# Latent and differential heads of a hybrid trunk on Trainium2: mask rows, packed values, rotation on GpSimd, and moved splits, evictions and fills

## The reference, cut to what matters

```python
# latent heads (B): keys of 64 + 32 dimensions, values of 64
s = (einsum(q_nope, k_nope) + einsum(q_rope, k_rope)) * scale
p = softmax(where(k_chunk <= q_chunk, s, -inf))      # chunks of 64 frames
out_b = einsum(p, v)
# differential heads (A): two score maps, values of 128
q, k = rope(rms_norm(q), pos), rope(rms_norm(k), pos)
p = softmax(s1) - lam * softmax(s2)                  # both masked by chunk
out_a = rms_norm(einsum(p, v)) * (1 - lam0)
x = x + concat(out_a, out_b) @ w_out
```

## Time and profile before

| | us |
|---|---|
| median of three executions | 1278.57 |
| lowest and highest | 1277.1, 1279.0 |
| profiled execution | 1279.58 |
| its span, first to last instruction | 1277.8 |
| TensorE busy | 1253.7 |
| ScalarE busy | 583.9 |
| VectorE busy | 569.3 |
| GpSimd busy | 528.7 |

### The profile page before, as it was taken

How to read it: one execution, slowest core, us unless ns; L and a number is a source line. 1 busy time by engine, 2 the same in 40 slices (tenths; PEclk the granted TensorE clock), 3 DMA queues, 4 the chain that set the end, 5 groups by cost and what they waited for, 6 DMA issues and landing times.

```text
span 1277.8 us, 16943 instructions
## 1 busy us (share of the span) xinstructions
PE 1253.7 (98%) x6308; PEld 1064.7 (83%) x6308; DVE 569.3 (45%) x995; ACT 583.9 (46%) x959; POOL 528.7 (41%) x267
## 2 busy tenths in 40 slices
PE   8999989999999999999999999999999999999999
PEld 8899968888888888888878888887888888888887
DVE  7856568553221022222288887887232210122210
ACT  5767756454322122223377878885443221222320
POOL 4656411175445344445432222222744444344442
PEclk9999989999999999999999999999999999999999
DMA  5221100033333222232221111110332332222331
GB/s 204 88 66 51 51 34 19 15 128 101 97 117 114 71 95 97 90 123 94 74 66 50 49 49 66 61 55 17 115 99 99 106 119 75 96 92 92 118 118 42
DMA packets 29143, 105.84 MB, mean 83 GB/s; under 512 B 3360, under 2 KB 3616, under 8 KB 29088
## 3 DMA queue, kind: packets, MB, share of 16 engines
q1 hardware_dynamic: 28944, 105.07, 24.8%
q10 hardware_dynamic: 144, 0.02, 0.0%
HBM read 102.98 MB, written 2.10 MB: 82 GB/s over the span
## 4 chain that ended last, share of the span: by engine, by line
PE 88%; DVE 8%; ACT 1%; issue 1%; POOL 1%; DMA 0%; POOLq 0%
PE bank L346 23%; PE bank L347 22%; PE bank L350 22%; PE bank L1512 3%; PE bank L1543 2%; PE bank L1459 1%; PE bank L1125 1%; PE bank L966 1%; PE bank L970 1%; PE bank L968 1%; PE bank L1074 1%; PE bank L1364 1%; PE bank L1365 1%; PE bank L1054 1%; PE bank L372 1%
## 5 line engine op out<-in xcount | busy, mean ns | idle before, releaser
L335 POOL TENSOR_TENSOR w_lo<-wraw,w_hi 128x1024 fp32r<-128x1024 f32 (+4 forms) x180 | 456.8, 2539 | 687.1 <-ACT w_hi L323 687.1
L346 PE MATMUL bank<-h_hi,w_hi 128*128 128x512 f32 x896 | 350.9, 392 | 0.1
L347 PE MATMUL bank<-h_lo,w_hi 128*128 128x512 f32 x896 | 349.0, 389 | 0.0
L323 ACT ACTIVATE w_hi<-wraw 128x1024 fp32r<-128x1024 f32 (+4 forms) x180 | 198.2, 1102 | 243.6 <-DVE x L671 125.6
L350 PE MATMUL bank<-h_hi,w_lo 128*128 128x512 f32 x896 | 221.8, 389 | 0.0
L346 PEld LDWEIGHTS bank<-h_hi,w_hi 128*128 128x128 f32 x896 | 168.2, 188 | 36.2 <-issue 1.1
L350 PEld LDWEIGHTS bank<-h_hi,w_lo 128*128 128x128 f32 x896 | 168.2, 188 | 34.9
L347 PEld LDWEIGHTS bank<-h_lo,w_hi 128*128 128x128 f32 x896 | 168.3, 188 | 34.3
L346 PE MATMUL bank<-f_hi,w_hi 128*128 128x512 f32 x352 | 136.9, 389 | 0.0
L347 PE MATMUL bank<-f_lo,w_hi 128*128 128x512 f32 x352 | 136.9, 389 | 0.0
L634 ACT ACTIVATE f_hi<-fa 128x512 f32 (+1 forms) x44 | 27.8, 633 | 217.2 <-DVE fa L660 217.2
(11 more groups left out here) (281 smaller groups left out, 1995.6 us busy)
## 6 DMA issues: line engine op xcount, KB each, us to landing
wraw<-in_w_in SPq DMA_DIRECT2D x120, 512.0 KB, 3.2
wraw<-in_w_down SPq DMA_DIRECT2D x32, 704.0 KB, 4.1
wraw<-in_w_ab SPq DMA_DIRECT2D x20, 512.0 KB, 3.3
x<-in_xt SPq DMA_DIRECT2D x8, 256.0 KB, 6.0
out<-x SPq DMA_DIRECT2D x8, 256.0 KB, 2.0
wraw<-in_w_ab SPq DMA_DIRECT2D x4, 416.0 KB, 6.0
wraw<-in_w_ab SPq DMA_DIRECT2D x2, 384.0 KB, 3.1
wraw<-in_w_ab SPq DMA_DIRECT2D x2, 256.0 KB, 2.8
```

Of the source, the lines that this page charges most:

```text
L323: nc.scalar.activation(whi[:, s, at:at + width], wraw[:, s, at:at + width], ACT.Copy).then_inc(S("w_hi"), 1)
L335: nc.gpsimd.tensor_tensor(wlo[:, s, at:at + width], wraw[:, s, at:at + width], whi[:, s, at:at + width], ALU.subtract).then_inc(S("w_lo"), 1)
L346: nc.tensor.matmul(out_bank, w, src_hi[kt], start=(kt == 0), stop=False)
L347: nc.tensor.matmul(out_bank, w, src_lo[kt], start=False, stop=False)
```

## The change

Masks: `masks_a` gets a second part of 512 columns in partitions 96 to 127. Of the 32, eight rows hold, on the query side, 1 where the frame is in chunk c and, on the key side, -1e30 where the key's chunk is later than c. They are written once into the spare partitions of `bqhi` and `bkhi` (zeros into those of `bqlo` and `bklo`), the latent scores contract over 128 rows instead of 96, and the four mask matmuls of a head are gone. The differential heads keep theirs.

Packed values: `vb` holds for each head 64 high columns beside 64 low ones. The first matmul gives high x high in output rows 0 to 63 and low x high in 64 to 127, the second adds high x low to rows 0 to 63. ScalarE copies the lower half to `bo`, VectorE adds the upper, and the sum is split from `bo` one head later.

Rotation: ScalarE squares and copies a projected half from the accumulator; VectorE only sums the squares; GpSimd makes all three products and the add (`qk_rope_pool`), in heads 1, 3, 5, 6. Both halves of a group are now evicted in the same head, for the value groups too. The differential transposes wait for all four rotations. `k_scale_pool` runs in heads 5 and 7.

Differential heads: zero fills on GpSimd in head 7, `T_L0` on ScalarE (`a_l0_act`), the split of chunk 22 + u after the transposed probabilities.

```diff
-    (vbhi, vblo), _ = pair("vb", [P, NB, B_HEADS * B_V])
+    vb, _ = place("vb", [P, NB, B_HEADS, 2 * B_V], F32R)
...
+    bo, end = place("bo", [P, SEQ], F32, at=r0)
...
-            act.wait_ge(S("cmask"), 1)
+            act.wait_ge(S("cmask"), 5)
...
-        c = slice(256 * hf, 256 * hf + 256)
-        nc.scalar.activation(vbhi[:, i, c], bank[KV_BANK[n % 3]][:, 256:512], ACT.Copy)
+        nc.scalar.activation(vb[:, i, 4 * hf:4 * hf + 4, 0:B_V],
+                             bank[KV_BANK[n % 3]][:, 256:512].rearrange("p (h n) -> p h n", h=4), ACT.Copy)
...
-        nc.vector.tensor_tensor(vblo[:, i, c], b[:, 256:512], vbhi[:, i, c], ALU.subtract).then_inc(S("bv_lo"), 1)
+        heads = slice(4 * hf, 4 * hf + 4)
+        nc.vector.tensor_tensor(vb[:, i, heads, B_V:2 * B_V], b[:, 256:512].rearrange("p (h n) -> p h n", h=4),
+                                vb[:, i, heads, 0:B_V], ALU.subtract).then_inc(S("bv_lo"), 1)
...
+        nc.scalar.activation(qk_of(p)[0][:, p % 2, 2 * t:2 * t + 2, :],
+                             bank[PJ[t]][:].rearrange("p (i n) -> p i n", i=2), ACT.Copy).then_inc(S("pj_c"), 1)
...
-    def qk_dve(dve, p, t):
-
+    def qk_sum_dve(dve, p, t):
+
+        dve.wait_ge(S("pj_sq"), 2 * p + t + 1)
+        nc.vector.reduce_sum(col(t_as(p) + 8 * t, 8), pj_sq[:, t, :].rearrange("p (j n) -> p j n", n=A_DIM),
+                             AX).then_inc(S("pj_sum"), 1)
...
+    ROPE_AT = (1, 3, 5, 6)
+
+    def qk_rope_pool(pool, p):
         dst, tab = qk_of(p)
...
+        o = dst[:, p % 2, :, :].rearrange("p i (j n) -> p i j n", n=A_DIM)
+        u = t2[:].rearrange("p (i j n) -> p i j n", i=NB, n=A_DIM)
...
-        nc.vector.tensor_tensor(u[:, :, :, 0:s], y[:, :, :, s:2 * s], of(A_DIM, s), ALU.mult)
-        nc.vector.tensor_tensor(u[:, :, :, s:2 * s], y[:, :, :, 0:s], of(A_DIM + s, s), ALU.mult)
-        nc.vector.tensor_tensor(o, y, of(0, A_DIM), ALU.mult).then_inc(S("pj_c"), 1)
-        nc.vector.reduce_sum(col(t_as(p) + 8 * t, 8), pj_sq[:, t, :].rearrange("p (j n) -> p j n", n=A_DIM),
-                             AX).then_inc(S("pj_sum"), 1)
...
-    def qk_add_pool(pool, p):
+            return spread(tab[:, :, a:a + w].rearrange("p i (j n) -> p i j n", j=1), [P, NB, 4, w])
         pool.wait_ge(S("pj_c"), 2 * p + 2)
-        dst, _ = qk_of(p)
-        o = dst[:, p % 2, :, :].rearrange("p i n -> p (i n)")
-        nc.gpsimd.tensor_tensor(o, o, t2[:], ALU.add).then_inc(S("pj_add"), 1)
+        wait(pool, "pj_add", p)
+        nc.gpsimd.tensor_tensor(u[:, :, :, 0:s], o[:, :, :, s:2 * s], of(A_DIM, s), ALU.mult).then_inc(S("pj_t"), 1)
+        nc.gpsimd.tensor_tensor(u[:, :, :, s:2 * s], o[:, :, :, 0:s], of(A_DIM + s, s), ALU.mult).then_inc(S("pj_t"), 1)
+        pool.wait_ge(S("pj_t"), 3 * p + 2)
+        nc.gpsimd.tensor_tensor(o, o, of(0, A_DIM), ALU.mult).then_inc(S("pj_t"), 1)
+        pool.wait_ge(S("pj_t"), 3 * p + 3)
+        nc.gpsimd.tensor_tensor(o, o, u, ALU.add).then_inc(S("pj_add"), 1)
...
+            pe.wait_ge(S("cmask"), 5)
...
             for n, (a, c) in enumerate(((bqhi, bkhi), (bqhi, bklo), (bqlo, bkhi))):
-                nc.tensor.matmul(o, a[0:B_QK, b * P:(b + 1) * P], c[0:B_QK, 0:w], start=(n == 0), stop=False,
-                                 skip_group_check=True)
-            last = nc.tensor.matmul(o[:, w - 256:w], ident_r[:], cmask[:, 0 if b == 0 else 1, :], start=False,
-                                    stop=True, skip_group_check=True)
+                last = nc.tensor.matmul(o, a[:, b * P:(b + 1) * P], c[:, 0:w], start=(n == 0), stop=(n == 2),
+                                        skip_group_check=True)
...
     def b_values_pe(pe, u, kb):
         pe.wait_ge(S("h_plo"), 3 * u + min(kb + 1, 3))
         if kb == 0:
-            wait(pe, "h_mlo", u)
-        c = slice(P * (u // 2), P * (u // 2) + P)
-        for n, (a, t) in enumerate(((vbhi, pthi), (vbhi, ptlo), (vblo, pthi))):
-            last = nc.tensor.matmul(bank[OUT][:, TQ[kb]:SEQ], a[:, kb, c], t[:, V_AT[kb]:V_AT[kb] + TW[kb]],
-                                    start=(kb == 0 and n == 0), stop=(kb == NB - 1 and n == 2))
+            wait(pe, "b_add", u)
+        for n, (rows, t) in enumerate(((P, pthi), (B_V, ptlo))):
+            last = nc.tensor.matmul(bank[OUT][0:rows, TQ[kb]:SEQ], vb[:, kb, u, 0:rows],
+                                    t[:, V_AT[kb]:V_AT[kb] + TW[kb]], start=(kb == 0 and n == 0),
+                                    stop=(kb == NB - 1), skip_group_check=True)
         if kb == NB - 1:
             last.then_inc(S("h_o"), 1)
 
-    def b_out_act(act, u):
+    def b_rows(u):
+        return slice(64 * (u % 2), 64 * (u % 2) + 64)
+
+    def b_lower_act(act, u):
         act.wait_ge(S("h_o"), u + 1)
-        r = slice(64 * (u % 2), 64 * (u % 2) + 64)
-        nc.scalar.activation(mhi[r, A_HEADS + u // 2, :], bank[OUT][r, :], ACT.Copy).then_inc(S("h_mhi"), 1)
-
-    def b_out_dve(dve, u):
+        wait(act, "h_mlo", u - 1)
+        nc.scalar.activation(bo[b_rows(u), :], bank[OUT][B_V:P, :], ACT.Copy).then_inc(S("b_lower"), 1)
+
+    def b_add_dve(dve, u):
+        dve.wait_ge(S("b_lower"), u + 1)
+        r = b_rows(u)
+        nc.vector.tensor_tensor(bo[r, :], bank[OUT][0:B_V, :], bo[r, :], ALU.add).then_inc(S("b_add"), 1)
+
+    def b_mhi_act(act, u):
+        act.wait_ge(S("b_add"), u + 1)
+        r = b_rows(u)
+        nc.scalar.activation(mhi[r, A_HEADS + u // 2, :], bo[r, :], ACT.Copy).then_inc(S("h_mhi"), 1)
+
+    def b_mlo_dve(dve, u):
         dve.wait_ge(S("h_mhi"), u + 1)
-        r = slice(64 * (u % 2), 64 * (u % 2) + 64)
-        nc.vector.tensor_tensor(mlo[r, A_HEADS + u // 2, :], bank[OUT][r, :], mhi[r, A_HEADS + u // 2, :],
+        r = b_rows(u)
+        nc.vector.tensor_tensor(mlo[r, A_HEADS + u // 2, :], bo[r, :], mhi[r, A_HEADS + u // 2, :],
                                 ALU.subtract).then_inc(S("h_mlo"), 1)
...
+                pe.wait_ge(S("a_zero"), 4)
...
-        if c == 2:
-            l0 = tiny[:, T_L:T_L + 8:2]
-            nc.vector.scalar_tensor_tensor(col(T_L0, NB), l0, EPS, l0, ALU.mult, ALU.mult).then_inc(S("a_l0"), 1)
+
+    def a_l0_act(act, u):
+        act.wait_ge(*at_a("e", 8 * u + 8))
+        nc.scalar.activation(col(T_L0, NB), tiny[:, T_L:T_L + 8:2], ACT.Square, scale=EPS ** 0.5).then_inc(S("a_l0"), 1)
...
-                pe.wait_ge(S("h_mlo"), B_HEADS)
+                pe.wait_ge(S("b_add"), B_HEADS)
...
-        pe.wait_ge(S("pj_add"), u // 2 + 1)
+        pe.wait_ge(S("pj_add"), 4)
...
-    def a_zero_dve(dve):
-
-        dve.wait_ge(S("h_s"), 3 * B_HEADS)
-        for t in (aqhi, aqlo):
-            nc.vector.memset(t[64:128, 0, :].bitcast(F32), 0.0)
-            nc.vector.memset(t[0:64, 1, :].bitcast(F32), 0.0)
+    def a_zero_pool(pool):
+
+        pool.wait_ge(S("h_s"), 3 * B_HEADS)
+        pool.wait_ge(S("pj_add"), 4)
+        pool.wait_ge(S("w_lo"), 14 + B_HEADS - 1)
+        for n, t in enumerate((aqhi, aqlo)):
+            nc.gpsimd.memset(t[64:128, 0, :].bitcast(F32), 0.0).then_inc(S("a_zero"), 1)
+            pool.wait_ge(S("a_zero"), 2 * n + 1)
+            nc.gpsimd.memset(t[0:64, 1, :].bitcast(F32), 0.0).then_inc(S("a_zero"), 1)
+            pool.wait_ge(S("a_zero"), 2 * n + 2)
...
+            sp.dma_start(rawm[:, :, 0:256], masks_a[:, :, 0:256]).then_inc(S("masks_in"), 16)
+            sp.dma_start(rawm[B_QK:P, :, 256:], masks_a[B_QK:P, :, 256:]).then_inc(S("masks_in"), 16)
...
-            qk_add_pool(pool, 0)
...
             for u in range(B_HEADS):
                 if u % 2 == 0 and u < 6:
                     b_pair_pool(pool, u // 2 + 1)
+                if u in ROPE_AT:
+                    qk_rope_pool(pool, ROPE_AT.index(u))
+                if u == B_HEADS - 1:
+                    a_zero_pool(pool)
                 lo(14 + u)
                 if u == 1:
                     rs_newton_pool(pool, "q0", 16, Z_Q)
                     rs_newton_pool(pool, ("k0", "k1")[u // 4], 16, Z_K + 16 * (u // 4))
                 elif u == 7:
                     rs_newton_pool(pool, "q1", 16, Z_Q + 16)
-                if u == 0:
-                    qk_add_pool(pool, 1)
-                elif u in (2, 4):
-                    qk_add_pool(pool, 1 + u // 2)
-                elif u in (3, 5):
-                    k_scale_pool(pool, (u + 1) // 2)
+                if u in (5, 7):
+                    k_scale_pool(pool, u // 2)
...
             for u in range(B_HEADS):
-                if u in (2, 4):
-                    qk_act(act, 1 + u // 2, 1)
-                if u == 6:
-                    va_act(act, 4, 1)
                 if u:
-                    b_out_act(act, u - 1)
+                    b_lower_act(act, u - 1)
                 b_exp_act(act, u, 0)
                 b_exp_act(act, u, 1)
                 b_exp_act(act, u, 2)
...
                     a_qk_act(act, 0)
                 for c in range(3):
                     b_pt_act(act, u, c)
+                if u:
+                    b_mhi_act(act, u - 1)
```

(45 more changed lines are left out.)

19 lines of the change are left out of this document (5 added, 14 removed).

## The result

The changed kernel takes 1268.18 us (median of four runs, 1268.0 to 1269.42), the kernel before 1278.78 on the same chip (four runs, 1277.1 to 1279.0): a ratio of 0.992 with a 95% interval of [0.9906, 0.9935], 10.6 us less. Forecast were 1266.0 us and a range of 1262.5 to 1271.0. The profiled execution is the slowest of the four, 1269.42 us, with a span of 1267.0. Its span is 10.8 us shorter than the profiled one of before; almost all of that (10.5 us) lies before the second differential head starts.

The account below looks back on a forecast made before the run. TensorE, busy 98% of the span, was taken as the bound. The terms summed to -13.1 us, giving 1266.5 from the profiled 1279.58 or 1265.5 from the median 1278.57; forecast 1266.0, range 1262.5 to 1271.0.

Parts of the forecast that it names:

- TensorE columns, -9.0: Latent heads: mask rows save 0.48 us and packed values 0.65 per head, -9.0 us over 8 heads.
- ScalarE late, +0.9: Latent heads 2, 4 and 6: ScalarE's extra copies and evictions make probabilities late, 0.3 us each, +0.9.
- Four rotations before head 7's transposes, +0.3: First differential head's transposes, in latent head 7, wait for all four GpSimd rotations: +0.3 us, bounds 0 and 1.5.
- Fills, -1.7: Latent head 7: zero fills moved from VectorE to GpSimd remove a stall of 1.7 us.
- head 0, -0.4: Latent head 0: of its 0.7 us over other heads, behind products before its first maximum, 0.4 goes.
- The shared port, +0.9: VectorE steps with two SBUF inputs wait under GpSimd reads: 0.2 us in three heads, 0.3 in head 7.
- the port decides: Rival, chance 0.13: two or three two-input VectorE steps wait a full 2.4 us, +5, giving 1271 us.
- Differential head 0, -4.6: First differential head falls from 22.4 to 17.5 to 18 us, 2.2 of the gain hanging on the clock.
- Prelude, +0.5: Prelude: ScalarE gets two copies, VectorE loses about 3 us; gain up to 1, loss up to 2.
- the clock falls again: Rival, chance 0.20: first differential head's clock falls, 2.2 us comes back, total -10.9, 1268.2 us.

Follow-up runs that it names:

- e3: Changed kernel with the four mask matmuls of a latent head back and 96 contraction rows: 1270.08 us.
- e5: Changed kernel with the packing of the values undone, three matmuls per key block as before: 1266.39 us.
- e10: e9 with ScalarE's copy of the high part moved out of latent heads 1, 3 and 5 to the next head's end: 1264.13 us.
- e7: Changed kernel with VectorE's means and low parts moved into its idle gap after the last reciprocal: 1266.46 us.
- e1: Changed kernel with the mean and root of head 6 moved into head 7: 1266.21 us.
- e8: Kernel before with only the tiny step on ScalarE and the split after the transposed probabilities: 1275.38 us.
- e9: e7 with differential head 0 reordered: two maxima ahead of value low parts and add, last key scaling behind the split: 1265.5 us.
- e11: e9 with the packing of the values undone: 1266.71 us.
- e2: Changed kernel with the fourth rotation left out, one 16-element GpSimd step in its place: 1267.92 us.
- e4: Changed kernel with the differential heads' tiny step back on VectorE and the weight split back ahead: 1269.44 us.

## Why the prediction was right, and which step failed

The time came out 2.2 us over the forecast and inside the range, as a faster kernel, and what the prediction named as signs of being right came true: heads of 10.67 us without mask rows, rotations of 7.4 us, a first differential head near 17.5 with no stretch at half clock. That is not because every term held.

- **TensorE columns, -9.0.** Both prices are right where TensorE is the bound: 0.49 for the masks (e3, head 0) and 0.68 for the values (11.35 in e5 against 10.67), forecast 0.48 and 0.65. The plain heads take 10.67 to 10.69. The sum was not collected in all eight heads: undoing the masks costs 1.9 us, not 3.8.
- **ScalarE late, +0.9.** Right in place and cause (e10), too small in size: heads 2, 4 and 6 are 0.57, 0.55 and 0.79 over 10.67, together 1.9.
- **Four rotations before head 7's transposes, +0.3.** Priced rightly on GpSimd (1.30, 1.29, 2.40 and 2.40 us; the stride costs nothing), and the last one ended at 148.93, before the transposes at 149.75 wanted it: nothing.
- **Fills, -1.7, and head 0, -0.4.** Head 0 went from 12.3 to 10.67, columns of 1.1 and some 0.5. The fills cost GpSimd 0.52 us each and nobody else anything; once head 7 is clear of the other stall it takes 11.14 (e7).
- **The shared port, +0.9: this is the step that failed.** I had put 0.3 in head 7 and measured 3.2 of the 3.7 us there, 2.3 of it the mean (e1) and 0.9 the low part (e7). Elsewhere it was small, as forecast: the mean takes 1.00 us in head 1 (that head is 0.17 longer, and not so in e7) and 0.40 in heads 3 and 5 (nothing). The prediction named the low part of head 6 as the exception and named the mean. What it missed is that both stand one behind the other there, each under a GpSimd instruction of its own, so the lateness adds up; that the mean of head 6 stands ahead of the first maximum, not in mid-head as in heads 1, 3 and 5; and that ScalarE's root waits for this mean with the lower half and the exponentials in its queue. In e5, where the mean waits for one instruction only and the heads are 0.68 longer, it costs nothing. Its rival "the port decides", two or three waits of 2.4 us for +5, is what happened in head 7, though in a smaller size: two waits, by 1.6 and 2.1 us over the steps' usual times, of which 3.2 reached TensorE.
- **Differential head 0, -4.6.** It gave 4.67, from 22.43 to 17.76. The blocked tiny step, the split and the clock carry 4.1 of it in the profile (e8), some 2 of that the clock, as forecast. The key scale made the scale of the second maximum take 0.91 us, 0.75 over its usual time, where I took 1.3.
- **Prelude, +0.5.** It became shorter: the first head starts at 71.01 instead of 71.42 (70.56 in e8, with the prelude of before), and in executions in which the clock keeps 1.00 there at 69.4 to 70.4 (e1, e3 to e7, e9, e11). In the profiled execution of the change it fell to 0.83 over 60 to 70 us (last row of the table above), which fits this run being 1.2 us over the other three.

In sum, the port and ScalarE were some 3.5 us too low. The prelude gave back 0.9 of that in the profiled execution and about 2 in the others (an estimate, with their 1.2 us), a gain that my term did not expect. That the total fell so near the forecast is in part luck. The missed term does not show in the total: it shows in the table by head.

**The rival "the clock falls again"** did not come true in the change: the clock is 1.00 in differential head 0 of the profiled execution, and its mean is 1.000 in the other three. Its price is right: in the kernel before the fall costs about 2 us (e8). At a mean clock of 1.000 the kernel before takes 1276.6 to 1277.1 us and the change 1268.0 to 1268.2, so some 8.7 of the 10.6 us are there without the clock.

**Open.** When the clock falls is not settled. Around TensorE's waits of 0.75 and 1.3 us it fell in differential head 0 in e1 and e7 and did not in the change and in e2; with waits of 0.18 and 1.86 it fell in e9 and not, with 0.18 and 1.87, in e10. It costs 0.65 to 0.75 us there. In e3 and e4 it fell in head 7 instead (mean 0.89), around waits of 2.0 and 2.5 us for the probabilities, and in the change it did not after 2.5.

## What to carry to other kernels

Moving elementwise work to GpSimd frees VectorE, but each long GpSimd instruction that reads SBUF can hold a VectorE step with both inputs in SBUF, however tiny (4 and 16 elements a row here). Put such steps where VectorE waits for another engine anyway, never right ahead of the first step of the next stage, and look at what other engines keep queued behind the one that reads them. Where columns are taken off the bounding engine, count them only in the stages in which it remains the bound, and check by a table per stage.

## What the runs showed of the hardware

- A VectorE step of 128x16 elements with SBUF inputs took 0.16 us alone, 2.24 and 2.34 us under GpSimd instructions of 2.84 and 2.39 us (change and e2), and 1.00 us under one of 1.30 (change, head 1). Each ended 0.03 or 0.04 us after that instruction. The prediction's reading of the Trainium skill, SBUF — State Buffer, section "SBUF: two separate sides", agrees with these rows: who has the pair keeps it for the whole instruction. A step with a PSUM input stays at its usual 0.67 to 0.69 us under the same GpSimd work (the add L1144 in e1, 0.68 us at 149.61, while the split ran from 148.25 to 151.10).
- A GpSimd fill did not hold it: in e1 the mean took 0.16 us at 151.28 while a fill of 0.52 us ran from 151.24.
- The wait goes both ways: the split issued at 148.88, when the low part had just been let through, took 2.84 us instead of the 2.39 to 2.49 of the others. So the low part, the split and the mean went one after the other, in the order of their coming.
- The same gaps in TensorE's work were followed by the lower clock in one execution and not in another: after waits of 0.18 and 1.86 us the granted clock was 0.50 from 166 to 168 us in e9, and after 0.18 and 1.87 it stayed at 1.00 in e10.
